# A second of the eight convolution tiles computed off TensorE, on GpSimd

## The reference, cut to what matters

```python
def conformer_conv(h, w_pw1, b_pw1, w_dw, b_dw, ln_g, ln_b, w_pw2, b_pw2):
    a = h @ w_pw1 + b_pw1
    u = a[..., :D_MODEL] * jax.nn.sigmoid(a[..., D_MODEL:])
    u = lax.conv_general_dilated(u, w_dw[:, None, :].astype(u.dtype), window_strides=(1,),
                                 padding=[(CONV_WIDTH - 1, 0)],
                                 dimension_numbers=('NWC', 'WIO', 'NWC'),
                                 feature_group_count=D_MODEL) + b_dw
    uf = u.astype(jnp.float32)
    mu = jnp.mean(uf, axis=-1, keepdims=True)
    var = jnp.mean(jnp.square(uf - mu), axis=-1, keepdims=True)
    u = ((uf - mu) * lax.rsqrt(var + EPS) * ln_g + ln_b).astype(h.dtype)
    return jax.nn.silu(u) @ w_pw2 + b_pw2
```

## Time and profile before

| | |
|---|---|
| three timed runs | 1044.61, 1045.42, 1049.27 us, median 1045.42 |
| span of the profiled execution | 1044.5 us |
| own time of the profiled execution | not listed apart; the median lies 0.9 us above its span |
| mean granted clock of TensorE | 0.997 |
| PE busy | 1019.3 us, 98% of the span |
| DVE busy | 665.9 us, 64% |
| ACT busy | 511.7 us, 49% |
| POOL busy | 65.5 us, 6% |
| DMA | 187.10 MB, mean 179 GB/s |

### The profile page before, as it was taken

How to read it: one execution, slowest core, us unless ns; L and a number is a source line. 1 busy time by engine, 2 the same in 40 slices (tenths; PEclk the granted TensorE clock), 3 DMA queues, 4 the chain that set the end, 5 groups by cost and what they waited for, 6 DMA issues and landing times.

```text
span 1044.5 us, 16429 instructions
## 1 busy us (share of the span) xinstructions
PE 1019.3 (98%) x7040; PEld 884.0 (85%) x7048; DVE 665.9 (64%) x759; ACT 511.7 (49%) x588; POOL 65.5 (6%) x83
## 2 busy tenths in 40 slices
PE   9999999999999999999999999999999999999997
PEld 7996788888988886988989897899658878888886
DVE  6565478676768776768877666254589865444544
ACT  5567564344346325654444444455477454343434
POOL 0000100000000000001001000000247000000000
PEclk9999999999999999999999999999999999999999
DMA  7542358667674762458888775323000445555541
GB/s 275 203 163 81 135 200 285 225 227 247 210 242 162 229 181 71 162 200 301 285 295 282 268 261 204 112 82 121 1 1 2 169 155 175 188 188 176 198 161 41
DMA packets 33613, 187.10 MB, mean 179 GB/s; under 512 B 3728, under 2 KB 7568, under 8 KB 14992
## 3 DMA queue, kind: packets, MB, share of 16 engines
q1 hardware_dynamic: 25488, 155.08, 42.8%
q0 software_dynamic: 7200, 27.27, 7.3%
q10 hardware_dynamic: 864, 3.88, 1.0%
HBM read 181.09 MB, written 1.05 MB: 174 GB/s over the span
## 4 chain that ended last, share of the span: by engine, by line
PE 85%; DVE 6%; ACT 4%; DMA 3%; issue 2%; DVEq 0%; SPq 0%; ACTq 0%
PE PS L277 11%; PE PS L603 11%; PE PS L604 11%; PE PS L605 11%; PE PS L279 11%; PE PS L278 11%; DMA raw<-wstream 3%; PE PS L1122 2%; ACT w_hi L260 2%; PE PS L636 1%; DVE w_lo L264 1%; PE PS L1356 1%; PE PS L1278 1%; PE PS L1056 1%; PE PS L1276 1%
## 5 line engine op out<-in xcount | busy, mean ns | idle before, releaser
L264 DVE TENSOR_TENSOR w_lo<-raw,w_hi 128x2048 fp32r<-128x2048 f32 x138 | 316.1, 2291 | 191.3 <-ACT w_hi L260 191.1
L260 ACT ACTIVATE w_hi<-raw 128x2048 fp32r<-128x2048 f32 x140 | 267.3, 1911 | 156.8 <-PE PS L279 80.6
L603 PE MATMUL PS<-w_hi,a_hi 128*128 128x512 f32 x512 | 203.3, 397 | 0.0
L604 PE MATMUL PS<-w_lo,a_hi 128*128 128x512 f32 x512 | 199.8, 390 | 0.0
L605 PE MATMUL PS<-w_hi,a_lo 128*128 128x512 f32 x512 | 199.8, 390 | 0.0
L277 PE MATMUL PS<-a_hi,w_hi 128*128 128x256 f32 (+1 forms) x512 | 155.0, 303 | 0.4 <-DVE a_lo L463 0.4
L278 PE MATMUL PS<-a_lo,w_hi 128*128 128x256 f32 (+1 forms) x512 | 151.7, 296 | 0.0
L279 PE MATMUL PS<-a_hi,w_lo 128*128 128x256 f32 (+1 forms) x512 | 151.6, 296 | 0.0
L277 PE MATMUL PS<-h_hi,w_hi 128*128 128x256 f32 x528 | 149.6, 283 | 0.7 <-DVE h_lo L797 0.7
L279 PE MATMUL PS<-h_hi,w_lo 128*128 128x256 f32 x528 | 149.4, 283 | 0.0
L278 PE MATMUL PS<-h_lo,w_hi 128*128 128x256 f32 x528 | 149.4, 283 | 0.0
(11 more groups left out here) (352 smaller groups left out, 1239.7 us busy)
## 6 DMA issues: line engine op xcount, KB each, us to landing
raw<-wstream SPq DMA_DIRECT2D x141, 1024.0 KB, 4.9
modraw<-wmod POOLq DMA_DIRECT2D x48, 512.0 KB, 4.9
U<-CU SPq DMA_DIRECT2D x28, 142.0 KB, 2.8
cst<-cst ACTq DMA_DIRECT2D x1, 1632.0 KB, 9.3
mlw<-mlw ACTq DMA_DIRECT2D x1, 1280.0 KB, 5.4
X<-xT SPq DMA_DIRECT2D x2, 512.0 KB, 5.2
raw<-wstream SPq DMA_DIRECT2D x2, 512.0 KB, 7.4
CROW<-crow POOLq DMA_DIRECT2D x1, 1024.0 KB, 5.2
```

The lines of the kernel that those rows point to most:

```text
L260: nc.scalar.activation(w_hi[:, slot, :], raw[:, rslot, :], ACT.Copy).then_inc(S("hi_done"), 1)
L264: dve.tensor_tensor(w_lo[:, slot, :], raw[:, rslot, :], w_hi[:, slot, :].bitcast(F32), ALU.subtract).then_inc(S("lo_done"), 1)
L603: nc.tensor.matmul(out, a_hi[:, k, src, ts], wh, start=k == 0, stop=False, skip_group_check=True)
L604: nc.tensor.matmul(out, a_hi[:, k, src, ts], wl, start=False, stop=False, skip_group_check=True)
```

## The change

Two tiles are now left off PE: tile 0 on DVE as before and tile 1 on POOL. PE convolves tiles 2 to 7. POOL gets 31 multiplications of 128x256 by a weight for each channel and 30 additions, each waiting for the one before on the semaphore `cv_tap_pool`; they stand in POOL's queue between the two `mod_tiles` calls. The sum tile of POOL is HN[:, 1], its term is SQ[:, 7]. Several semaphores of the first layer (`glr_mm`, `gate_mm`, ...) become one, `gla_mm`, with thresholds 1 to 7, which frees numbers and moves no instruction. The places that count with ON_DVE count with PLAIN.

```diff
-ON_DVE = 1
+ON_DVE, ON_POOL = 1, 1
+PLAIN = ON_DVE + ON_POOL
+POOL_OPS = 2 * TAPS - 1
...
-                if U_PW1 + 4 + ON_DVE <= u < U_PW1 + 4 + KT:
+                if U_PW1 + 4 + PLAIN <= u < U_PW1 + 4 + KT:
                     packed(u - U_PW1 - 4)
...
-                if j >= ON_DVE + 2:
+                if j >= PLAIN + 2:
                     conv(j - 2)
             conv(6)
-            for k in range(ON_DVE, KT - 1):
-                pe.wait_ge(S("cv_read"), k + 1 - ON_DVE)
-                nc.tensor.matmul(PS[:, 6, 0:T], ones, HN[:, k, :], start=k == ON_DVE, stop=False)
+            for k in range(PLAIN, KT - 1):
+                pe.wait_ge(S("cv_read"), k + 1 - PLAIN)
+                nc.tensor.matmul(PS[:, 6, 0:T], ones, HN[:, k, :], start=k == PLAIN, stop=False)
             pe.wait_ge(S("cv_tap"), ON_DVE * (TAPS + 1))
-            for k in range(ON_DVE):
-                i = nc.tensor.matmul(PS[:, 6, 0:T], ones, HN[:, k, :], start=False, stop=k == ON_DVE - 1)
+            pe.wait_ge(S("cv_tap_pool"), ON_POOL * POOL_OPS)
+            for k in range(PLAIN):
+                i = nc.tensor.matmul(PS[:, 6, 0:T], ones, HN[:, k, :], start=False, stop=k == PLAIN - 1)
...
                 if k < 2:
-                    taps_laid(ON_DVE + k)
+                    taps_laid(PLAIN + k)
...
-                if k >= ON_DVE + 2:
+                if k >= PLAIN + 2:
                     taps_laid(k)
...
             dve.wait_ge(S("cv_tap"), ON_DVE * (TAPS + 1))
-            dve.wait_ge(S("cv_read"), 7 - ON_DVE)
+            dve.wait_ge(S("cv_tap_pool"), ON_POOL * POOL_OPS)
+            dve.wait_ge(S("cv_read"), 7 - PLAIN)
...
             mod_tiles(2, 18)
+
+            for k in range(ON_DVE, PLAIN):
+                total, term = HN[:, k, :], SQ[:, 6 + k, :]
+                pool.wait_ge(S("cu_done"), k + 1)
+                for j in range(TAPS):
+                    moved, w = CU[:, k, j:j + T], prm("wdw", 32 * k + j)
+                    if j == 0:
+                        pool.tensor_scalar(total, moved, w, prm("bdw", k), ALU.mult, ALU.add)\
+                            .then_inc(S("cv_tap_pool"), 1)
+                    else:
+                        pool.wait_ge(S("cv_tap_pool"), POOL_OPS * (k - ON_DVE) + 2 * j - 1)
+                        pool.tensor_scalar(term, moved, w, None, ALU.mult).then_inc(S("cv_tap_pool"), 1)
+                        pool.wait_ge(S("cv_tap_pool"), POOL_OPS * (k - ON_DVE) + 2 * j)
+                        pool.tensor_tensor(total, total, term, ALU.add).then_inc(S("cv_tap_pool"), 1)
+
             mod_tiles(18, MODB)
```

More of the change, by code:

```diff
@@ L876, in half @@
             return slice(64 * e, 64 * e + 64)
+        GLA_MM = {"ranks": 1, "factors": 2, "gate": 3, "keys": 4, "updates": 5, "outputs": 6, "sums": 7}
         block = ctx.enter_context(nc.Block())
@@ L892, in packed @@
                 sp.wait_ge(S("cu_done"), k + 1)
-                if k >= ON_DVE + 4:
-                    sp.wait_ge(S("conv_done"), k - 3 - ON_DVE)
+                if k >= PLAIN + 4:
+                    sp.wait_ge(S("conv_done"), k - 3 - PLAIN)
                 for g in range(4):
@@ L920, in _ @@
                                      stop=k == KT - 1)
-            i.then_inc(S("glr_mm"), 1)
+            i.then_inc(S("gla_mm"), 1)
             def first_sums():
@@ L990, in _ @@
                                      GLR, start=True, stop=True)
-            i.then_inc(S("gate_mm"), 1)
+            i.then_inc(S("gla_mm"), 1)
             in1(6)
@@ L999, in _ @@
                                             KEND[:, a * T + t * P:a * T + (t + 1) * P], ident)
-            i.then_inc(S("ktok_mm"), 1)
+            i.then_inc(S("gla_mm"), 1)
             in1(8)
@@ L1011, in _ @@
                         start=True, stop=True)
-            i.then_inc(S("upd_mm"), 1)
+            i.then_inc(S("gla_mm"), 1)
             in1(9)
@@ L1022, in _ @@
                                          start=True, stop=True)
-            i.then_inc(S("og_mm"), 1)
+            i.then_inc(S("gla_mm"), 1)
             qk_ss(0)
@@ L1114, in conv @@
             def conv(k):
[L1116 to L1119, removed]
+                pe.wait_ge(S(f"u4_loaded{k % 4}"), 64 * (k // 4 + (k % 4 >= PLAIN)))
+                pe.wait_ge(S("w4_built"), k + 1 - PLAIN)
+                if k >= PLAIN + 4:
+                    pe.wait_ge(S("cv_read"), k - 3 - PLAIN)
                 for q in range(8):
@@ L1532, in _ @@
                     hi(act, u + 3)
-            act.wait_ge(S("gate_mm"), 1)
+            act.wait_ge(S("gla_mm"), GLA_MM["gate"])
             for a in range(2):
@@ L1569, in _ @@
             hi(act, 13)
-            act.wait_ge(S("og_ss"), 1)
+            act.wait_ge(S("gla_mm"), GLA_MM["sums"])
             nc.scalar.activation(OR, banks(0, 2), ACT.Ln, scale=1.0 / P, bias=prm_eps).then_inc(S("og_rs"), 1)
@@ L1642, in _ @@
                     ctx_squares(act)
-                if j >= ON_DVE + 3:
+                if j >= PLAIN + 3:
                     conv_read(j - 3)
@@ L1942, in _ @@
                 lo(dve, u + 3)
-            dve.wait_ge(S("gate_mm"), 1)
+            dve.wait_ge(S("gla_mm"), GLA_MM["gate"])
             dve.wait_ge(S("gate_read"), 1)
@@ L1965, in _ @@
             copy_proj(8)
-            dve.wait_ge(S("upd_mm"), 1)
+            dve.wait_ge(S("gla_mm"), GLA_MM["updates"])
             dve.wait_ge(S("gla_exp"), 2)
@@ L2132, in _ @@
                 without(ks)
-            dve.wait_ge(S("cv_read"), KT - ON_DVE)
+            dve.wait_ge(S("cv_read"), KT - PLAIN)
             without(slice(7, 8))
@@ L2514, in _packed_taps @@
     packed = w.reshape(8, 4, KT, 4, 32).transpose(4, 1, 2, 3, 0).reshape(P, 256)
-    plain = [w[:, k * P:(k + 1) * P].T for k in range(ON_DVE)]
-    return np.concatenate(plain + [packed[:, 32 * ON_DVE:]], 1)
+    plain = [w[:, k * P:(k + 1) * P].T for k in range(PLAIN)]
+    return np.concatenate(plain + [packed[:, 32 * PLAIN:]], 1)
 def _constants():
```

14 lines of the change are left out of this document (7 added, 7 removed).

## The result

| | before | changed |
|---|---|---|
| median of four runs | 1045.96 us | 1064.87 us |
| the same without the run of 2580.9 us | | 1063.85 us |
| span of the profiled execution | 1044.5 us | 1061.9 us |
| mean granted clock | 0.997 | 0.989 |
| PE / DVE / POOL busy | 1019.3 / 665.9 / 65.5 us | 1019.7 / 673.8 / 131.6 us |

The ratio is 1.0171, with a 95% interval from 1.0154 to 1.0188: slower by 1.7%. One of the four runs of the changed kernel took 2580.9 us, which no trace explains; it is left out of the ratio, which belongs to the 1063.85 us of the other three. The profiled execution took 1063.85 us as well. The forecast was 1051.1 us within 1043 to 1063: the sign is right, the time lies just above the range, and it is close to the 1064 us of rival 2.

The account below looks back on a forecast made before the run. PE, busy 98% of the span, was taken as the bound, with DVE close behind. DVE's lateness lets PE begin the last tile at 408.1 us against 402.42: 1045.4 + 5.7 = 1051.1 us, range 1043 to 1063 us.

Parts of the forecast that it names:

- rival 2: POOL's own chain, not DVE, holds PE if a step costs over 0.65 us; at 0.85 us, 1064 us; chance 0.28.
- What leaves PE and DVE: One convolved tile off PE, 3.59 us, with 0.15 us given back at unit 4; one W4 build off DVE, 1.14 us.
- the 1042.0 worked out: Rival of a clean gain: DVE and POOL fill each other's gaps, PE is never held, 1042.0 us; chance 0.13.
- What POOL gets: 31 multiplications at 0.39 us, 30 additions at 0.515 us and 61 gaps of 0.16 us on POOL: 37.4 us alone.
- the upper bound: Upper limit for POOL's 256-column multiplication, taken from the two-input addition's 0.515 us.
- the stops: Time DVE holds SBUF against POOL, 29.3 us, less 6.4 us of overlapping steps; POOL then ends at 405 us.
- What POOL and DVE cost each other: SBUF sharing delays 37 DVE instructions by 0.28 us each, 10.4 us, so DVE's plain tile ends at 407.2 us.
- Taps over 0.6 us: Sign of a right forecast: DVE's taps have a mean over 0.6 us in place of 0.478.
- Low halves were to grow: Sign of a right forecast: DVE's low halves grow by some 0.3 us.
- PE's clock: PE's granted clock was to stay at its upper level, 2.4 GHz; no cost was put on it.
- the sign that the forecast gave for it: POOL releasing PE's wait with DVE done at 400 us or sooner would show POOL's chain as the last.

Follow-up runs that it names:

- Experiment 1: Changed kernel with POOL doing only the first term of tile 1, its other 60 steps left out of the output: 1042.87 us, ratio 0.9969.
- experiment 9: Kernel of experiment 6 with DVE's two running sums moved from SBUF to an unused PSUM bank: 1052.32 us, ratio 1.0054.
- experiment 7: Changed kernel with ACT making tile 1's 30 products, five in each of rounds 2 to 7; POOL keeps first term and additions: 1056.18 us, ratio 1.009.
- experiment 6: Changed kernel with a second operation, an addition of 0.0, in each of POOL's 30 multiplications: 1056.63 us, ratio 1.0102.
- experiment 3: Changed kernel with POOL doing 16 of tile 1's 31 taps, the other 15 left out of the output: 1047.87 us, ratio 1.0013.
- experiment 5: Changed kernel with 70 products of zeros on PE, into an unused bank, ahead of its wait for POOL: 1062.46 us, ratio 1.015.
- Experiments 4: Changed kernel with POOL's same 61 steps ordered as four multiplications in a row, then their four additions: 1062.51 us, ratio 1.0152.

## Why the prediction was wrong, step by step

**What leaves PE and DVE: right.** 3.59 us, less what comes back at unit 4. Experiment 1 gives 1042.87 us against the 1042.0 worked out, and a wait of unit 4 of 0.2 us against 0.15. In the change this wait was 0.80 us. The low half itself took 2.29 us as before; it began late, since POOL had slowed DVE's instructions ahead of it (the low half before it took 2.52 us, the first tap 0.82 in place of 0.41).

**What POOL gets: the step that failed.** The multiplication was taken as 0.39 us, the middle between half a memset and an addition of 0.515 us. It takes 0.92 us, above the upper bound. The bound rested on the thought that one input cannot cost more than two, and the trace of before had no row of the operation to bear that out. The addition was taken as half of a 512-column one, 0.515 us; it takes 0.72 us, so half the columns did not mean half the time. The gap was 0.09 us against 0.16. Alone that is 55.5 us against 37.4, or 0.91 us a step: some 16 us more for the multiplications, 6 us more for the additions, 4 us less for the gaps. Rival 2 needed over 0.65 us a step. For the stops the forecast had 29.3 - 6.4 = 22.9 us and the trace has 15.9. So POOL's end: 405.1 + 18.1 - 7.0 - 0.5 (an earlier start) = 415.7 us, which is the measured one. The forecast had DVE as the later engine, by 2 us; it was POOL, by 10.7 us.

By the rule of the Trainium skill that one-input work runs at roughly line rate (GPSIMD Engine Reference, Engine selection) the multiplication would have been, as an estimate, 0.26 us. The row refutes this for the form with one operation, which is dearer than the two-input addition; the form with two, at 0.48 us, is nearer. The rule gave the same 0.26 us as half a memset, and I weighed both as a possible gain only. For the other half of that rule, two-input work at about half of DVE's speed, the forecast said that its row agrees. That was read too kindly: 1.03 us against DVE's 0.68 us for 512 columns is 1.5 times as long. For 256 columns it is 0.72 against 0.42 us, 1.7 times.

**What POOL and DVE cost each other: right in kind, a little too dear.** 10.4 us were forecast, and DVE's tile came at 404.98 us: 8.2 us on the forecast's own count (404.98 - 396.8). Taps over 0.6 us were asked for; they are 0.66. The parts are not alike, though: 29 taps lost 0.18 us each, four builds of `W4` 0.53 us, seven low halves 0.09 us and the last addition 0.41 us, some 8.4 us together. So one loss for every DVE instruction holds only as a mean of this mixture. The loss depends on what meets: none for a tap with a PSUM input (experiment 9), 0.47 us a tap beside back-to-back additions (experiment 7), 0.3 us beside the faster multiplications (experiment 6). Low halves were to grow by some 0.3 us.

**PE's clock: the second step that failed.** The forecast said that the granted clock stays at 2.4 GHz, because the trace of before had no wait of this length in the stage. A missing row is not a row of zero, and its cost should have stood as a bound. In the windows of the changed kernel from 399 us on it was (columns as above):

```profile
399.00:415.80 16.80, 0.22 (x2) 0.00 (x0) 5.95 (x8) 0.64 (x1) 15.26 (x17) 0.62 0.24 78
415.80:417.90 2.10, 2.04 (x8) 1.25 (x12) 0.00 (x0) 0.00 (x0) 0.00 (x0) 0.50 0.00 0
417.90:420.20 2.30, 2.30 (x24) 1.07 (x28) 1.75 (x3) 1.41 (x3) 0.00 (x0) 0.54 0.00 0
420.20:422.50 2.30, 2.30 (x45) 1.11 (x37) 0.48 (x2) 1.12 (x3) 0.00 (x0) 1.00 0.03 7
```

Two sums and half a tile ran at 1.2 GHz: 1.14 + 1.05 = 2.2 us. Had POOL's prices been right, PE would still have waited, and the clock might have cost some 3 us more, as in the trace of experiment 3.

**The sum, mended.** Forecast +5.7 us. POOL's end instead of DVE's: 415.7 - 407.2 = 8.5 us. PE's first sum begins 0.15 us after it. The clock 2.2 us. Together 5.7 + 8.5 + 0.15 + 2.2 = 16.5 us, the shift of the chain. So 2.2 us of it are the clock's, and experiment 5 gives them back; the rest is the wait for POOL. The other 0.9 us of the span lie outside this stage and are less than the runs differ from each other.

**The range.** Rival 2 was named, with its mechanism, its place and a time of 1064 us, and got 0.28. Its mechanism came true, but that its 1064 us were met so closely is in part luck: it had POOL end at 420 us, 4.3 us too late, since the stops were put 7 us too high and the step at 0.85 us was 0.06 too short, and it had no term for the clock. Nor was DVE done at 400 us or sooner, the sign that the forecast gave for it; DVE was late too, at 404.98 us. The range ended at 1063 us although the rival's price had no upper bound from any row. With two of three prices unmeasured it should have gone further: on the forecast's own scale of 6 us for 0.1 us, 0.95 us a step is 1070 us.

Left open: why the multiplication with one operation takes twice as long as the one with two. Experiments 4 and 6 show that it is the form and not the order; what POOL does inside it no run here tells. Also untested is another order on PE, with the last tile's convolution ahead of the two sums and their wait.

## What to carry to other kernels

Before work goes to an idle engine, get one row of each instruction that it would execute, in its exact form: 60 dependent steps turn a mistake of 0.3 us into 18 us, and a neighbouring operation is not a bound. Ask which instructions of the two engines will meet, and move one input of the neighbour to PSUM before judging the idea. And price a wait of the bounding engine with what its clock loses behind it: in one trace here 3 us of waiting cost 6.

## What the hardware showed that was not expected

- On POOL a 128x256 multiplication by a weight for each partition takes 0.92 us, and 0.48 us when a second operation, the addition of 0.0, is in the same instruction.
- POOL's instructions that a DVE instruction stops do not appear as waits: they grow (from 0.92 to 3.04 us beside a low half, and from 0.48 to 3.45 us in experiment 6). Only the duration tells.
- A faster POOL made DVE slower: with the multiplication at 0.48 us DVE's tile came 4.4 us later. In experiment 7 four taps in a row beside POOL's additions lasted 0.94 us each in place of 0.47.
- Behind a wait of PE of 3.1 us the granted clock was 0.50 in the traced execution, which cost another 3.05 us. In the changed kernel 70 products of zeros ahead of the wait kept it at 1.00.
